# A chain of transformer blocks on one core: gated linear attention with its newest level first in each engine's order, and other matmuls among the last head's levels

## The reference, cut to what matters

```python
def _gla_chunkwise(q, k, v, lf, S):          # 16 heads, key and value width 128
    def step(S, xs):
        qc, kc, vc, lfc = xs
        b = jnp.cumsum(lfc, axis=2)
        o = jnp.einsum('bhtk,bhkv->bhtv', qc * jnp.exp(b), S)
        pair = jnp.exp(jnp.where(tri, b[:, :, :, None, :] - b[:, :, None, :, :], -jnp.inf))
        a = jnp.einsum('bhtk,bhtsk->bhts', qc, pair * kc[:, :, None, :, :])
        o = o + jnp.einsum('bhts,bhsv->bhtv', a, vc)
        ...
def _c_mixer(h_lat, h_ctx, w_in, lb, h_norm, w_out, need_ctx):
    q, f_fwd, f_bwd, i, z = _split_cols(h @ w_in, C_SIZES)     # 2048 columns each
    f = lb + (1.0 - lb) * jax.nn.sigmoid(f_pre)                # k = 1 - f, lf = log(f)
    o_l, o_c = _gla_bidir(rec_l, rec_c, need_ctx)              # both directions, summed
    o = _rms(o, h_norm)                                        # per head
    return (o * jax.nn.silu(z)) @ w_out
x = x + gate * y_lat
```

## Time and profile before

| | |
|---|---|
| median of 3 runs | 4201.51 us (4199.68 to 4202.0) |
| the profiled execution | 4205.8 us |
| its span, first to last instruction | 4204.0 us |
| mean granted TensorE clock | 0.98 |
| gate tiles | 1441.6 to 1553.2 us |
| heads 0 to 14 with the projection of the next | 1591 to 2436 us, some 56.8 us each |
| last head alone | 2436.3 to 2498.95 us |
| output tiles | 2498.95 to 2610.6 us |

### The profile page before, as it was taken

The page is one execution under the profiler, slowest core; times in us unless marked ns, Lnnn a source line. Parts: engine busy times, 40 slices in busy tenths (PEclk is TensorE's granted clock), DMA queues, the critical chain, the costliest instruction groups (busy, mean ns, idle before and its releaser), DMA issues.

```text
span 4204.0 us, 38947 instructions
## 1 busy us (share of the span) xinstructions
PE 3968.8 (94%) x15382; PEld 2323.1 (55%) x15382; DVE 1490.1 (35%) x2687; ACT 1245.4 (30%) x2311; POOL 884.2 (21%) x885
## 2 busy tenths in 40 slices
PE   7999999999989999999999969998999889999998
PEld 3555555665555546766666654444666644444443
DVE  2433422222220105666666641346666610010000
ACT  3444442222220213444444420674444310000000
POOL 0000000100000004556655540233343410000000
PEclk9999999999999999999999979999999989999999
DMA  5121012011011121111101101220110002212211
GB/s 198 47 81 43 28 35 80 0 60 60 30 58 63 40 80 41 41 41 41 40 22 41 41 21 58 75 82 20 41 41 31 31 33 80 93 62 79 74 69 48
DMA packets 23045, 225.74 MB, mean 54 GB/s; under 512 B 2512, under 2 KB 5072, under 8 KB 7376
## 3 DMA queue, kind: packets, MB, share of 16 engines
q1 hardware_dynamic: 22864, 223.25, 14.4%
HBM read 221.14 MB, written 2.10 MB: 53 GB/s over the span
## 4 chain that ended last, share of the span: by engine, by line
PE 75%; issue 9%; POOL 8%; DVE 4%; ACT 3%; DMA 1%; POOLq 0%; DVEq 0%; ACTq 0%; SPq 0%
PE bank L1335 7%; PE bank L1011 7%; PE bank L825 4%; PE bank L922 4%; PE bank L791 4%; PE bank L1346 4%; PE bank L1170 3%; PE bank L1039 3%; PE bank L983 3%; PE bank L777 3%; PE bank L1311 3%; POOL arena L2491 2%; POOL arena L2503 2%; PE bank L952 2%; PE bank L844 2%
## 5 line engine op out<-in xcount | busy, mean ns | idle before, releaser
L1049 PE MATMUL bank<-hT,ring 128*128 128x256 f32 (+1 forms) x1024 | 348.6, 487 | 0.1
L1335 PE MATMUL bank<-hT,ring 128*128 128x512 f32 x704 | 303.9, 595 | 2.4 <-DVE hT L1882 2.4
L1011 PE MATMUL bank<-Y,ring 128*128 128x512 f32 (+1 forms) x768 | 277.1, 524 | 3.0 <-DVE Y L2197 3.0
L1049 PEld LDWEIGHTS bank<-hT,ring 128*128 128x128 f32 x1024 | 187.6, 190 | 117.7 <-issue 101.4
L1335 PEld LDWEIGHTS bank<-hT,ring 128*128 128x128 f32 x704 | 134.3, 191 | 172.0 <-issue 170.7
L1659 ACT ACTIVATE arena<-arena 128x1024 f32<-128x1024 f32 x112 | 118.4, 1057 | 357.1 <-POOL arena L2491 357.1
L1011 PEld LDWEIGHTS bank<-Y,ring 128*128 128x128 f32 x768 | 146.4, 191 | 133.5 <-issue 123.1
L1170 PE MATMUL bank<-hT,ring 128*128 128x512 f32 x384 | 181.7, 609 | 14.2 <-ACT arena L1719 8.8
L1059 PE MATMUL bank<-ring,hT 128*128 128x128 f32 x1536 | 180.6, 276 | 13.9 <-ACT arena L1607 13.9
L825 PE MATMUL bank<-hT,ring 128*128 128x256 f32 (+1 forms) x512 | 186.5, 501 | 2.4 <-ACT hT L1412 2.4
L1059 PEld LDWEIGHTS bank<-ring,hT 128*128 128x128 f32 x1536 | 175.2, 192 | 20.0 <-ACT arena L1607 20.0
(11 more groups left out here) (400 smaller groups left out, 6928.5 us busy)
## 6 DMA issues: line engine op xcount, KB each, us to landing
ring<-in_w SPq DMA_DIRECT2D x61, 2048.0 KB, 8.0
ring<-in_w SPq DMA_DIRECT2D x20, 1280.0 KB, 5.5
ring<-in_w SPq DMA_DIRECT2D x16, 1536.0 KB, 6.9
ring<-in_w SPq DMA_DIRECT2D x12, 1024.0 KB, 4.8
ring<-in_w SPq DMA_DIRECT2D x8, 1408.0 KB, 6.0
ring<-in_w SPq DMA_DIRECT2D x18, 512.0 KB, 3.6
xT<-in_xT SPq DMA_DIRECT2D x1, 3072.0 KB, 12.3
out<-arena SPq DMA_DIRECT2D x1, 2048.0 KB, 6.2
```

Of the source, the lines that this page charges most:

```text
L1011: ins = e.matmul(m[:, 0:b - a], w[:, k, sl(j % 2)], src[:, k, a:b], start=k == 0, stop=k == kt - 1)
L1049: ins = e.matmul(m[:, 0:b - a], w[:, k, sl(1 + d)], hT[:, k, a:b], start=k == 0, stop=k == 7)
L1335: ins = e.matmul(m, w[:, k, sl(2 * i + j % 2)], hT[:, k, 0:LAT], start=k == 0, stop=k == 7)
```

## The change

In the attention's pipeline, each tick now has the newest job's step first, so that within a tick e of a level stands ahead of x of the one before, then m, then a, and at the turn between heads the second direction's transposes (`gl_t`) stand ahead of the first one's states (`gl_u`) and of the output of the head before. Gate tile 15 is taken out of the gate stage (its weights are a slab of their own, `zc1`) and becomes four groups `zc_` in the ticks of the last head, with its Silu (`zcs`) and a load of the exp and log table behind it. Seven eighths of output tiles 0 and 1 (k 0 to 13, 14 groups `oc_`) follow in the last head's ticks; the last two k of both tiles stay behind the heads, ahead of tiles 2 to 7.

```diff
-def pipeline(jobs):
+def pipeline(jobs, newest=False):
...
-                made += group
+                made[0 if newest else len(made):0 if newest else len(made)] = group
...
+def gl_last():
+
+    return ([[("zc_", c)] + [("zcs",), ("tables",)] * (c == 3) for c in range(4)]
+            + [[("oc_", j, c)] for j in range(2) for c in range(7)])
...
-    heads = pipeline(gl_jobs())
+    heads = pipeline(gl_jobs(), True)
     for j in range(16):
         side = iter(gl_project(j + 1) if j < 15 else [])
+        if j == 15:
+            side = iter(gl_last())
         for n in range(11):
             made += next(side, []) + next(heads)
-            for _ in range(1 if n < 9 else 2):
+            for _ in range((1 if n < 9 else 2) if j < 15 else n in (3, 6)):
                 made += next(side, [])
-        for group in side:
-            made += group
+        if j < 15:
+            for group in side:
+                made += group
     for group in heads:
+        made += group + next(side, [])
+    for group in side:
         made += group
...
-         + [("oab", j) for j in range(8)] + [("tables",)] + norm_sums(1) + norm_rest(1) + [("zc", j) for j in range(16)]
-         + [("tables",), ("gl_bound",)] + gl_steps() + [("oc", j) for j in range(8)]
+         + [("oab", j) for j in range(8)] + [("tables",)] + norm_sums(1) + norm_rest(1) + [("zc", j) for j in range(15)]
+         + [("tables",), ("gl_bound",)] + gl_steps() + [("oc_", 0, 7), ("oc_", 1, 7)] + [("oc", j) for j in range(8)]
...
+            def zc_(c):
+                if c == 0:
+                    slab("zc1", 8)
+                    take(proj, ("zc", 15, 0), ("zc_silu", (15, 0)))
+                w, m = open_w["zc1"][0], bank[spot["zc", 15, 0]]
+                for k in (2 * c, 2 * c + 1):
+                    ins = e.matmul(m, w[:, k, :], hT[:, k, 0:LAT], start=k == 0, stop=k == 7)
...
             def oc(j):
-                if j == 0:
+                if j >= 2:
+                    out("oc", j, 16, yc, BOTH[:1])
+
+            def oc_(j, c):
+                if c == 0:
+                    if j == 0:
+                        slab("oc", 16)
+                    take(proj, ("oc", j, 0), ("oc_x", (j, 0)))
+                    q.wait_ge(*on("gl_out", 13))
+                if c == 7:
                     q.wait_ge(*on("gl_out", 15))
-                out("oc", j, 16, yc, BOTH[:1])
+                w, m = open_w["oc"][0], bank[spot["oc", j, 0]]
+                for k in (2 * c, 2 * c + 1):
+                    ins = e.matmul(m, w[:, k, sl(j)], yc[:, k, :], start=k == 0, stop=k == 15)
```

More of the change, by code:

```diff
@@ L45 @@
 SIZE = {"ada0": 4096, "ada1": 4096, "zab": 1024, "na": 3072, "gate": 1024, "mqk": 4096, "mvo": 4096,
-        "oab": 4096, "zc": 4096, "gla": 4096, "oc": 4096, "rg": 2560, "dz": 2048, "ba": 1024, "dn": 3072,
+        "oab": 4096, "zc": 4096, "zc3": 3072, "zc1": 1024, "gla": 4096, "oc": 4096, "rg": 2560, "dz": 2048, "ba": 1024, "dn": 3072,
         "mixp": 2560, "mixg": 2048, "wo": 4096, "gu": 4096, "down": 2816}
 CUT = (["ada0"] * 6 + ["zab"] * 16 + ["na"] * 8 + ["gate"] + ["mqk", "mvo"] * 4 + ["oab"] * 4
-       + ["ada1"] * 6 + ["zc"] * 4 + ["gla"] * 16 + ["oc"] * 4 + ["rg"] * 12 + ["ba"] + ["dz"] * 4 + ["dn"] * 8
+       + ["ada1"] * 6 + ["zc"] * 3 + ["zc3", "zc1"] + ["gla"] * 16 + ["oc"] * 4 + ["rg"] * 12 + ["ba"] + ["dz"] * 4 + ["dn"] * 8
        + ["mixp", "mixg"] * 8 + ["wo"] * 2 + ["gu"] * 11 + ["down"] * 8)
@@ L381 @@
     "ml_p": lambda h, i, s, c: ["mqk"] * (i == s == c == 0), "ml_v": lambda h, i: ["mvo"] * (i == 4),
-    "oab": lambda j: ["oab"] * (j % 2 == 0), "zc": lambda j: ["zc"] * (j % 4 == 0),
-    "gl_q": lambda j, c: ["gla"] * (c == 0), "oc": lambda j: ["oc"] * (j % 2 == 0),
+    "oab": lambda j: ["oab"] * (j % 2 == 0), "zc": lambda j: ["zc3" if j == 12 else "zc"] * (j % 4 == 0), "zc_": lambda c: ["zc1"] * (c == 0),
+    "gl_q": lambda j, c: ["gla"] * (c == 0), "oc": lambda j: ["oc"] * (j % 2 == 0 and j > 0), "oc_": lambda j, c: ["oc"] * (j == c == 0),
     "rg_u": lambda j: ["rg"], "dz": lambda j, c: ["dz"] * (j % 2 == c == 0), "dn_gate": lambda: ["ba"],
@@ L798, in zc @@
                 if j % 4 == 0:
-                    slab("zc", 8)
+                    open_w["zc"] = (slab("zc3" if j == 12 else "zc", 8), opened[0] - 1)
                 z("zc", j, open_w["zc"][0], BOTH[:1], "zc_silu", 1)
+                if j == 14:
+                    give("zc", "zc_mm", (j, 0))
+            def zc_(c):
[5 more added lines that the diff above has]
+                    ins = e.matmul(m, w[:, k, :], hT[:, k, 0:LAT], start=k == 0, stop=k == 7)
+                if c == 3:
+                    ins.then_inc(up("zc_mm", (15, 0)), 1)
+                    give("zc1", "zc_mm", (15, 0))
             def dz(j, c):
@@ L1022, in oc @@
             def oc(j):
-                if j == 0:
-                    q.wait_ge(*on("gl_out", 15))
-                out("oc", j, 16, yc, BOTH[:1])
+                if j >= 2:
[7 more added lines that the diff above has]
+                if c == 7:
+                    q.wait_ge(*on("gl_out", 15))
+                w, m = open_w["oc"][0], bank[spot["oc", j, 0]]
+                for k in (2 * c, 2 * c + 1):
+                    ins = e.matmul(m, w[:, k, sl(j)], yc[:, k, :], start=k == 0, stop=k == 15)
+                if c == 7:
+                    ins.then_inc(up("oc_mm", (j, 0)), 1)
+                    if j:
+                        give("oc", "oc_mm", (j, 0))
             def gl_bound():
@@ L1348, in down @@
                 give("down", "down_mm", j)
-            do = {"start": start, "ada": ada_, "adat": adat, "ns": ns, "zab": zab, "zc": zc, "dz": dz, "na_p": na_p, "na_n": na_n,
+            do = {"start": start, "ada": ada_, "adat": adat, "ns": ns, "zab": zab, "zc": zc, "zc_": zc_, "dz": dz, "na_p": na_p, "na_n": na_n,
                   "na_v": na_v_, "na_vt": na_vt, "na_s": na_s, "na_t": na_t, "na_o": na_o, "ml_gate": ml_gate, "ml_gt": ml_gt,
                   "ml_p": ml_p, "ml_sw": ml_sw, "ml_s": ml_s, "ml_v": ml_v, "ml_bc": ml_bc, "ml_nd": ml_nd, "ml_o": ml_o, "ml_y": ml_y,
-                  "oab": oab, "oc": oc, "gl_bound": gl_bound, "gl_q": gl_q, "gl_f": gl_f, "gl_v": gl_v, "gl_t": gl_t,
+                  "oab": oab, "oc": oc, "oc_": oc_, "gl_bound": gl_bound, "gl_q": gl_q, "gl_f": gl_f, "gl_v": gl_v, "gl_t": gl_t,
                   "gl_u": gl_u, "gl_d1": gl_d1, "gl_m": gl_m, "gl_o": gl_o, "gl_n": gl_n, "rg_lam": rg_lam,
@@ L1824, in scalar @@
             do = {"start": start, "tables": tables, "ns": ns, "nr": nr, "nh": nh, "zabs": zabs,
-                  "zc": lambda j: z("zc", j, yc, BOTH[:1]), "dz": lambda j, c: c == 3 and z("dz", j, yd, BOTH[:1]), "na_sq": na_sq_,
+                  "zc": lambda j: z("zc", j, yc, BOTH[:1]), "zcs": lambda: z("zc", 15, yc, BOTH[:1]), "dz": lambda j, c: c == 3 and z("dz", j, yd, BOTH[:1]), "na_sq": na_sq_,
                   "na_rs": na_rs_, "na_vc": na_vc, "na_x": na_x, "na_t": na_t, "ml_gate": ml_gate, "ml_p": ml_p, "ml_s": ml_s, "ml_v": ml_v,
@@ L2751, in layout @@
     W += [slab(wa[1], (512 * s, 512 * s + 512)) for s in range(6)]
-    W += [slab(wc, (8192 + 512 * s, 8704 + 512 * s)) for s in range(4)]
+    W += [slab(wc, (8192 + 128 * a, 8192 + 128 * b)) for a, b in ((0, 4), (4, 8), (8, 12), (12, 15), (15, 16))]
     W += [slab(wc, *[(2048 * a + 128 * j, 2048 * a + 128 * j + 128) for a in range(4)]) for j in range(16)]
```

## The result

| | before | after |
|---|---|---|
| median | 4201.76 us (4 runs, 4199.68 to 4202.44) | 4095.31 us (4 runs, 4089.68 to 4100.84) |
| ratio | | 0.9747, 95% interval 0.9731 to 0.9764 |
| the profiled execution, its span | 4205.8, 4204.0 us | 4100.8, 4099.1 us |

A forecast was written before the change was run, and what follows sets the result against it. TensorE, busy 94% of the span, was taken as the bound. Savings of 42 (heads), 6.9 (gate tile) and 32.2 (last head and output), less 2 for clock, gave 79.1 us: median 4122 us, 8-in-10 range 4108 to 4158.

The forecast's parts named there:

- Heads 0 to 14: the failed step: Heads 0 to 14: newest level first removes 42 of 43.8 us of TensorE's listed waits (bounds 20 and 43.8).
- A level in the last head: Last head: GpSimd and VectorE taking turns need 2.28 + 1.26 = 3.54 us, taken as 3.6 a level; 4.65 means no gain.
- Last head and output tiles: From 2436.30 us, last head and output stage end after 142.1 us against 174.3: 32.2 us saved.
- the cover of 0.6 us: Turn between heads: second key transposes' keys ready at 2391.8, TensorE there at 2392.4; without this margin, 1 to 2 us a head.
- The gate tile: Gate stage: one TensorE-bound tile of 6.87 us removed there, 6.9 us saved.
- the count to 56.2: Last head: tick-by-tick count from 2436.30 us; last matmul group ends at 56.2 us, TensorE's work until then 50.9 us.
- The Silu and its tables: Last head, ScalarE: Silu and two table loads take 3.2 us, free before the first level exponential; uncovered, 1 to 2 us once.
- The clock: Last head's level ticks: a lower granted clock could cost 9 us over five ticks, or none; 2 us taken.
- the return of half of the waits: Rival: half the heads' waits return at the turn, or levels stay nearer 4.2 us; 4136 to 4158 us, chance 0.18.
- levels that get no quicker: Rival: VectorE and GpSimd obstruct each other, leaving only the moved matmuls' gain; 4170 us (4158 to 4180), chance 0.11.
- the loss by shared access: Rival: VectorE and GpSimd take turns for everything in a head; at 62 us a head, 4248 us, chance 0.03.

The follow-up runs named there:

- The light exponents in the old order: Kernel before, old step order, with both engines' exponent instructions of each level cut to one column: 4125.09 us in one execution, 816.48 us for the heads' stage.

## Why the prediction was wrong

**Heads 0 to 14: the failed step.** The step put TensorE's possible gain at the sum of its listed waits, 43.8 us, and took 42. The mechanism was right (the listed waits are gone, the vector side runs ahead, TensorE alone sets the pace), the size was not: 66.6 us. The sum should have been made of TensorE's own steps, start to start in stretches without any wait, not of "idle". The rows were there: in the trace before, eight 512-column records take 3.44 us from start to start in one place (2384.99 to 2388.43) and 3.69 in another (2411.09 to 2414.78), and a level product 0.89 in one place and 0.97 in another. I wrote "eight 512-column records in 3.4 to 3.6 us" and 0.93 for the product, and took the width of both for nothing. The missing 1.5 us a head are 0.22 and 0.26 us ahead of products 0 and 1, 0.16, 0.16 and 0.15 on top of the three listed waits, and 0.56 in small pieces. The light exponents in the old order show that, without waits of either kind, the old order's stage is the changed kernel's (816.48 and 816.52 us). I also called 43.8 an upper bound, so the range's lower end came from the same mistake: with 66.6 in its place the sum would have been 103.7 us and the forecast 4098.

**The other steps held, one of them by luck.**
- A level in the last head: 3.6 us forecast by turns, 3.57 measured. The sum is right, its terms are not. GpSimd's multiplies of keys take 0.72 us with VectorE idle (L2545 above, at 2392.62; 0.69 from start to start), where I had 0.57, and 0.14 us pass between two levels; so by estimate GpSimd alone needs 2 x 0.57 + 2 x 0.69 + 0.14 = 2.66 us and not 2.28, and VectorE's three instructions cost it the other 0.91 and not 1.26. The two errors cancel. And L2176's 0.42 us at 2452.12 is not "with GpSimd quiet": GpSimd's L2467 ran from 2452.28, and L2176 had only started first; L2177 behind it took 1.49.
- Last head and output tiles: count to 142.1 forecast, 142.60 measured. The second key transposes waited 1.0 us for L2500 (2371.72 on TensorE), as counted, and the last level product came 43.7 us into the head, where the count has 43.2; in heads 0 to 14 the cover of 0.6 us held. The output tiles from tile 2 on took 82.40 us, as counted with the two last groups.
- The gate tile: 6.9 us forecast in its own stage, 6.86 measured. The 8.55 of the table has 1.7 of clock in it. That four of the groups cost the last head 4.3 us by holding up the second state product was inside the count to 56.2, but I did not say it, and so did not see that the gate tile was worth 2.55 us.
- The Silu and its tables took the 3.2 us, and their cover held. They do hold up the first level exponential, by some 2.1 us (its last exponents are there at 2377.93, it starts at 2380.14), but it ends at 2381.20, and VectorE's multiply, which needs it, has its turn only at 2383.23. ScalarE's timeline after:

```profile
2376.93 1.28 ACT L1457 ACT_TABLE_LOAD   x1
2378.23 0.60 ACT L1457 ACTIVATE Y<-bank 128x512 f32<-128x512 f32 x1
2378.84 1.28 ACT L1421 ACT_TABLE_LOAD   x1
2380.14 1.06 ACT L1698 ACTIVATE arena<-arena 128x1024 f32<-128x1024 f32 x1
```

  The Trainium skill gives another 1.38 us of drain with each load ("ScalarE: Activation LUTs", What ACT_TABLE_LOAD costs). These lines show none, and neither do rows 9: the next activation starts 0.02 us behind each load. The measurement decides.
- The clock: 2 us set aside, none lost (1.00 in the last head).
- The rivals: none came true, not the return of half of the waits, nor levels that get no quicker, nor the loss by shared access. The shared access is real (0.9 us of GpSimd's time a level, by the estimate above), but TensorE has enough work of its own in heads 0 to 14 to cover it.

## What to carry to other kernels

When a wait of TensorE goes, more can go than its idle entry: price it by the spacing of starts of the same instructions in an undisturbed stretch, here 4.54 us a head instead of 3.03. In a software pipeline over in-order queues try the newest stage first in a tick; the exponential of the next step then lies beside the multiplies of this one, without an instruction added. And look where filler matmuls stand in a stretch that waits for a chain: the four groups ahead of the second state product, on which the chain hangs here, cost 4.3 of the 6.9 us that they brought.

## What the runs showed of the hardware that was not expected

- Where the first weights of a level product arrive late, and its load stands 0.03 to 0.07 us ahead of its matmul instead of 0.42, 0.22 to 0.26 us are lost without any idle time being shown on TensorE; behind a listed wait it is 0.15 to 0.16 us on top of the entry (0.56 for 0.40, 1.09 for 0.93, 1.85 for 1.70).
- Cutting an instruction of VectorE can lengthen one of GpSimd (0.79 to 1.06 us), when another of VectorE's moves beside it.
- TensorE's stages repeat to 0.03 us between executions where the clock is 1.00 (the heads 816.52, 816.52, 816.53 us in three executions of the changed kernel), while the whole program varies by 11 us.
